# Routing a mixture of experts: row stores between weight loads, and router logits on the two halves of TensorE's columns

## The reference, cut to what matters

```
g_prob   = softmax(h @ w_group + b_group)                  # 4 groups
g_top_p, g_top = top_k(g_prob, 1)
e_logits = (h @ w_expert + b_expert)[the chosen group]     # 8 of 32
e_top_p, e_top = top_k(softmax(e_logits), 2)
gate     = g_top_p * e_top_p
# each token goes to 2 experts; rows are sorted by expert into padded blocks;
# each block: y = (silu(x @ w1[e]) * (x @ w3[e])) @ w2[e]; results are weighted and summed
```

## Time and profile before

| what | value |
|---|---|
| median of 3 runs | 3810.07 us (3807.57 to 3821.53) |
| the profiled execution: its own time | 3816.75 us |
| its span, first to last instruction | 3814.6 us |
| PE busy | 3213.9 us (84%), 32538 instructions |
| PE weight loads | 2381.8 us (62%) |
| DVE busy | 1687.6 us (44%) |
| ACT busy | 875.3 us (23%) |
| POOL busy | 370.0 us (10%) |
| mean granted TensorE clock | 0.924 of full speed |
| DMA of SyncE's queue (q1) | 383.22 MB of 421.94 MB |

### The profile page before, as it was taken

One profiled execution on the slowest core, in us unless ns is written; L12 is line 12 of the kernel. 1 busy time (PEld: TensorE's weight loads), 2 busy tenths in 40 slices (PEclk: granted clock), 3 DMA queues, 4 the chain that ended last, 5 costly groups with the idle time before them and its releaser, 6 DMA issues. The chain is left out here.

```text
span 3814.6 us, 75665 instructions
## 1 busy us (share of the span) xinstructions
PE 3213.9 (84%) x32538; PEld 2381.8 (62%) x32538; DVE 1687.6 (44%) x3122; ACT 875.3 (23%) x1808; POOL 370.0 (10%) x530
## 2 busy tenths in 40 slices
PE   4899699995873899699895874889988989999998
PEld 0666499873542666598873542457656778878843
DVE  2234455443113344455443114535547776666611
ACT  3111322212113121322212113223344310022200
POOL 0000122001111000112001111000015400000000
PEclk8899799997996999799997996999999999999999
DMA  8210300107996210300107996110010032222221
GB/s 301 80 34 21 128 31 5 58 23 295 375 407 193 61 50 26 133 5 4 59 22 300 398 404 191 39 46 23 23 57 1 1 100 100 78 78 89 74 69 45
DMA packets 175280, 421.94 MB, mean 111 GB/s; under 512 B 25636, under 2 KB 122276, under 8 KB 146420
## 3 DMA queue, kind: packets, MB, share of 16 engines
q1 hardware_dynamic: 155987, 383.22, 27.2%
q0 software_dynamic: 8736, 17.32, 1.8%
q10 hardware_dynamic: 10240, 16.79, 1.3%
HBM read 400.55 MB, written 50.54 MB: 118 GB/s over the span
## 5 line engine op out<-in xcount | busy, mean ns | idle before, releaser
L2021 PE MATMUL ps<-e_w,e_xt 128*64 128x256 f32 x1792 | 226.9, 410 | 66.9 <-DMA e_w<-in_moe_w 65.0
L2021 PEld LDWEIGHTS ps<-e_w,e_xt 128*64 128x64 f32 x1792 | 149.6, 148 | 166.2 <-issue 78.0
L710 PE MATMUL ps<-h,win 128*128 128x264 f32 x960 | 233.2, 397 | 16.8 <-DVE pad L859 15.2
L2128 DVE TENSOR_TENSOR e_hid<-ps,e_silu 64x256 f32<-64x256 f32 x64 | 39.4, 616 | 416.7 <-ACT e_silu L2087 416.7
L710 PEld LDWEIGHTS ps<-h,win 128*128 128x128 f32 x960 | 180.8, 193 | 67.4 <-issue 38.6
L3511 PE MATMUL ps<-ff_up,wt 128*128 128x512 f32 x352 | 152.2, 592 | 0.0
L3451 PE MATMUL ps<-h_lat,wt 128*128 128x256 f32 x544 | 133.4, 388 | 15.2 <-DMA wt<-in_w_in 8.4
L1416 DVE COPY_PREDICATED inv<-level,ps 112x384 f32<-112x384 int32 x176 | 103.4, 587 | 90.8 <-PE ps L1317 82.4
L1317 PE MATMUL ps<-inv,nt 48*48 48x48 f32 x3520 | 130.8, 207 | 11.3 <-issue 10.3
L3451 PE MATMUL ps<-h_lat,w_sums 128*128 128x256 f32 x544 | 130.0, 382 | 0.0
L2040 PE MATMUL ps<-e_w,e_hid_t 128*64 128x512 f32 x448 | 112.8, 622 | 19.8 <-DMA e_w<-in_moe_w 15.7
(11 more groups left out here) (613 smaller groups left out, 6953.0 us busy)
## 6 DMA issues: line engine op xcount, KB each, us to landing
e_w<-in_moe_w SPq DMA_DIRECT2D x168, 1024.0 KB
wmod<-in_w_mod SPq DMA_DIRECT2D x24, 1024.0 KB, 14.1
early<-in_moe_w SPq DMA_DIRECT2D x24, 1024.0 KB, 15.0
wt<-in_w_up SPq DMA_DIRECT2D x22, 1024.0 KB, 5.0
y_rows<-e_y ACTq DMA_DIRECT2D x128, 128.0 KB
win<-in_w_in SPq DMA_DIRECT2D x10, 1536.0 KB, 6.6
wt<-in_w_in SPq DMA_DIRECT2D x12, 1024.0 KB, 5.0
wt<-in_w_down SPq DMA_DIRECT2D x16, 704.0 KB, 5.5
```

The lines of the kernel that those rows point to most:

```text
L710: last = pe.matmul(ps[:, 7, 0:HT], lhsT=ring[(s + 1) % 2][:, i, o:o + P], rhs=k.h[:, i, h * HT:(h + 1) * HT], start=(i == 0), stop=(i == K ...
L2021: last = pe.matmul(ps[half, 2 + z, 0:EH], lhsT=xt[z][:, f, :], rhs=w[:, f, :], start=(f == 0), stop=(f == KD - 1))
L2128: dve.tensor_tensor(hid[z][high, :].rearrange("s (t q) -> s q t", t=2), ps[high, 2 + z, 0:EH].rearrange("s (q t) -> s q t", t=2), si[z][hi ...
```

## The change

Two things are done.

1. In `route`, SyncE asks for expert 1's weights, stores rows 0, 1 and 2, asks for expert 2's weights, stores rows 3, 4 and 5, asks for expert 3's weights, and waits for the six stores.
2. In `mix_close`, both token halves go to PSUM bank 2: tokens 0 to 263 on output partitions 0 to 35, tokens 264 to 527 on output partitions 64 to 99 (N_B = 64). `router_b` is loaded twice, at partitions 0 and 64; the bias is added by two DVE operations of 264 tokens each in place of one of 528; `logits_t` is 100 partitions by 264. In `route` the six transposes of the logits take their input from the one or the other half and write three to bank 6 and three to bank 7; DVE reads both banks with one copy.

```diff
                 sp.dma_start(k.router[:, :, :], a["router"][bass.ds(li, 1), :, :].rearrange(
                     "a (t p) n -> p (a t) n", p=P)).then_inc(rest_in, 16)
-                sp.dma_start(k.router_b[:, :], a["router_b"][bass.ds(li, 1), :].rearrange("a n -> n a")
-                             ).then_inc(rest_in, 16)
+                for b in (0, N_B):
+                    sp.dma_start(k.router_b[b:b + NR, :], a["router_b"][bass.ds(li, 1), :].rearrange("a n -> n a")
+                                 ).then_inc(rest_in, 16)
...
-                sp.wait_ge(rest_in, 16 * 8)
+                sp.wait_ge(rest_in, 16 * 9)
...
                     for h in range(2):
-                        last = pe.matmul(ps[0:NR, 2 + h, 0:HT], lhsT=k.router[:, f, :],
+                        last = pe.matmul(ps[N_B * h:N_B * h + NR, 2, 0:HT], lhsT=k.router[:, f, :],
                                          rhs=k.h[:, f, h * HT:(h + 1) * HT], start=(f == 0), stop=(f == KD - 1))
...
                 dve.wait_ge(logits_made, 1)
-                dve.tensor_scalar(split2(k.logits_t[:, :]), ps[0:NR, 2:4, 0:HT], k.router_b[:, 0:1], None,
-                                  ALU.add).then_inc(logits_kept, 1)
+                for b in (0, N_B):
+                    dve.tensor_scalar(k.logits_t[b:b + NR, :], ps[b:b + NR, 2, 0:HT], k.router_b[b:b + NR, 0:1], None,
+                                      ALU.add).then_inc(logits_kept, 1)
...
-            for n in range(SOON, PRE):
-                load_early(k, a, li, sp, n)
+            load_early(k, a, li, sp, SOON)
             for j in range(NC1):
                 sp.wait_ge(kept, j + 1)
                 sp.dma_start(k.h_rows[j * TC:(j + 1) * TC, :], rows[:, j, :]).then_inc(stored, 16)
+                if j == 2:
+                    load_early(k, a, li, sp, SOON + 1)
+            for n in range(SOON + 2, PRE):
+                load_early(k, a, li, sp, n)
             sp.wait_ge(stored, 16 * NC1)
...
             for j in range(NC1):
-                o = ps[0:TC, 6, j * NR:(j + 1) * NR]
-                last = pe.transpose(o, k.logits_t[:, j * TC:(j + 1) * TC], k.ident[0:NR, 0:NR])
+                of = slice(N_B * (2 * j // NC1), N_B * (2 * j // NC1) + NR)
+                at = j % (NC1 // 2) * TC
+                last = pe.transpose(ps[0:TC, 6 + 2 * j // NC1, j % 3 * NR:(j % 3 + 1) * NR],
+                                    k.logits_t[of, at:at + TC], k.ident[of, of])
...
-            chain(dve.tensor_copy(lg[:, :, :], ps[0:TC, 6, 0:NC1 * NR].rearrange("p (j n) -> p j n", j=NC1)))
+            chain(dve.tensor_copy(lg[:, :, :].rearrange("p (b j) n -> p b (j n)", b=2),
+                                  ps[0:TC, 6:8, 0:NC1 // 2 * NR]))
...
-        k.router_b = k.sb("router_b", [NR, 1], stack=s1)
-        k.logits_t = k.sb("logits_t", [NR, T], stack=s1)
+        k.router_b = k.sb("router_b", [N_B + NR, 1], stack=s1)
+        k.logits_t = k.sb("logits_t", [N_B + NR, HT], stack=s1)
```

## The result

| | before | changed |
|---|---|---|
| median with the first result | 3812.59 us (6 runs) | 3793.86 us (6 runs) |
| ratio, 95% interval | | 0.9941 [0.9927, 0.9954] |
| span of the profiled execution | 3814.6 us | 3789.7 us |

Two later comparisons of the same pair, 0.9940 and 0.9944, are among the experiments. The forecast was 3792.2 us, a gain of 17.9 us; the medians differ by 18.7, the ratios say 21 to 23.

The account below looks back on a forecast made before the run. PE averaged 84% busy, but the prediction took router products before `route` and stores behind nine 1 MB loads as binding. Gains of 11.2 + 6.7 = 17.9 us from the 3810.07 median gave 3792.2 us; 8-in-10 range 3784 to 3802.

Parts of the forecast that it names:

- The order of the queue: In `route`, stores among the expert loads let `experts` start 6.29 us earlier in layer 0, 4.92 in layer 1: 11.2 us.
- The model: SyncE's queue in `route`, rebuilt from the old order's prices: release at 891.0, DVE's end at 892.03 in layer 0.
- no price for turning: SyncE's queue in `route`: load and store alternate without cost, as the old trace's one change of direction showed none.
- The first gather: Start of `experts`: gather moves along with the stage, still 8.0 us from issue to PE's first transpose, no gain or cost.
- Rival (b): Start of `experts`: first gather waits for the whole load backlog, costing 4.0 us a layer, 3800.2 us; chance 0.06.
- The router: Router products before `route` on two column halves: gains 3.47 and 3.49 us, less 0.28 for DVE, 6.7 us.
- ACT does bind where the clock is high early: Router products: with the clock high from the start ACT would bind, the two gains at most 1.2 us more in sum.
- The undersized term: DVE's bias after the router products: two operations take 0.90 us against 0.76, +0.14 a layer, bounds 0 and +0.3.
- The sum: Whole kernel: 11.2 us from the queue's order plus 6.7 us from the router, 17.9 us, giving 3792.2 us.
- The chances: Whole kernel: faster by over 0.5% 0.36, within 0.5% 0.61, slower by over 0.5% 0.03.
- the bound that I placed 1.2 us from the forecast: Whole kernel: 0.5%, 19.05 us, is what a measurement can tell from no change; the bound lies at 3791.0 us.

Follow-up runs that it names:

- router only: The changed kernel with the old loop over the early experts, so only the router's two halves against the kernel before; ratio 0.9971 [0.9962, 0.9980], 11.0 us.
- router on one half: The kernel before with both token halves of the router on output partitions 64 to 99, banks 2 and 3; router products took 8.84 and 8.74 us.
- bias in two: The kernel before with the bias added in two DVE operations of 264 tokens, partitions as before; the pair took 0.88 us.
- order only: The kernel before with only the new order of SyncE's queue in `route`, the router as before; ratio 0.9973 [0.9961, 0.9985], 10.3 us.

## Why the prediction was right, and where it was off

**The order of the queue: right.** The model (422 GB/s for loads, 1.31 us for a store, 1.65 and 2.1 us at the ends, no price for turning) put SyncE's release 26.7 us after the start of `route` in layer 0, from 864.28 to 891.0; measured 26.4. DVE became the next to be late, as said. The start of `experts`, mean over four old-order profiles and both layers (before, router only, router on one half, bias in two): 35.07 us after `route`. Over four new-order ones (three of the changed kernel and order only): 29.74. That is 5.33 a layer, **10.7 us** against 11.2. Two small terms differ: `experts` starts 1.50 us after DVE, not 1.67, and DVE's chain took 28.4 us, not 27.75, in most profiles. This second one goes with the clock. In layer 1 of the changed kernel the counting products ran when the granted clock fell to half, and DVE waited 0.7 us longer for them (the stretches of 1 us show PE, clock, share and GB/s):

```profile
1996.00:1997.00 1.00, 0.45 (x2) 0.70 0.96 373
1997.00:1998.00 1.00, 1.00 (x4) 0.50 0.93 365
...
1998.17 1.26 DVE L1853 TENSOR_TENSOR ahead<-ahead,ps 88x32 f32<-88x32 f32 x6 [1.67 <-PE ps L1767]
```

In layer 0 that wait was 1.0, and in both layers of before the chain took 27.75. Since DVE now ends the stage, this 0.7 us is on the path; before, the stores hid it.

**The first gather: a term taken as zero.** From the start of `experts` to the first transpose, the same eight and eight stretches: 11.28 before, 10.73 after. **1.1 us** in sum, not forecast. Rival (b), a gather behind the whole backlog, would have made it longer; it fell. Why it became shorter was not tried. It is as short with all stores first and with one expert ahead of them (means 10.82 and 10.72), where DVE ends `route` too, and longer where the stores still end it (10.97 with stores of 80 and 8 rows, 11.19 with a store behind every load, 11.39 on ACT's queue). It seems to go with what ends `route`.

**The router: right in mechanism, a little high.** From the first product to the start of `route`: 11.94 us over ten stretches with one half (before, order only, stores on ACT's queue, router on one half, stores of 80 and 8 rows), 8.87 over fourteen with two. 3.07 a layer, **6.1 us** against 6.7. In the profiled pair the products gained 3.50 in layer 0 (forecast 3.47) and 3.36 in layer 1 (3.49). In layer 0 the clock was at half for 5.68 us (0.83 in the stretch from 856) and at full for 0.86, together worth 3.70 us at full clock; the forecast had 3.79. ACT does bind where the clock is high early: in four profiles of layer 0 and three of layer 1 the products took 5.67 or 5.68, to a hundredth, whatever the clock's moment. The undersized term was the bias: 0.25 more in place of 0.14.

**The sum.** 10.7 + 1.1 + 6.1 = 17.9 us by stages, the forecast's own sum. That it is the same to a tenth is luck: the errors of its terms, 0.5 and 0.6 us too much and 1.1 too little, cancel. The timed ratios (0.9941, 0.9940, 0.9944) say 21 to 23. Each interval alone still reaches the 0.9953 of 17.9 us; three of them together make it likely that some 4 us more are real. The router alone, with 11.0 us [7.6, 14.5] timed and 6.1 by stages, points to where to look. No stretch of a profile shows it: the longest two outside these stages, from the start to `mix_close` of layer 0 and between the layers, average 746.7 and 726.6 us over the seven profiles with the new router, 747.6 and 726.3 over the six with the old one, against a scatter of 10 and 12 us. It stays open.

**The chances.** I gave 0.61 to a change under 0.5% and 0.36 to more; the three ratios lie at 0.56 to 0.60%, just beyond the bound that I placed 1.2 us from the forecast. The range 3784 to 3802 held it.

## What to carry to other kernels

Read which wait ends a stage last, and ask what stands ahead of it in the same queue: here 2 MB that the next stage needed stood behind 9 MB that it needed only later, and 5 to 6 us a layer came from reordering the requests alone. Leave no gap in doing so: the version that put the stores first of all started the next stage as early and still measured some 7 us slower, a third of the gain (likely real, not shown). And count the partitions of a transfer: with stores of 88 rows alone in the queue the DMA share was 0.68, 11 of 16 engines.

## What the runs showed of the hardware that was not expected

- Two queues on the same DMA engines moved packet for packet, 110 and 108 in 4 us, not byte for byte: ACT's 4 KB stores got 0.38 MB in 4 us beside SyncE's 1.3 MB, so six stores took over 20 us on a queue of their own and 7.9 in a row on SyncE's.
- Writes to DRAM from 88 partitions ran at 272 GB/s and a share of 0.68; cut into 80 and 8 rows, at 391 GB/s and 0.97 to 1.03. Among loads, the stretch at 0.69 came only after the last store had landed.
- A queue that alternates reads and writes eleven times lost nothing that can be seen: release at 31.0 us, 31.7 by the plain sum.
- Two DVE operations on the same 36 partitions took 0.88 us as a pair, on partitions 0 to 35 and 64 to 99 1.01 us.
